# A mixture-of-experts layer whose weights stream through a ring: the large and the small expert of a pair alternate unit by unit within a phase, and the down product waits for its groups of tokens one by one

## The reference, cut to what matters

```
def swiglu(h, w_gate, w_up, w_down):
    return (jax.nn.silu(h @ w_gate) * (h @ w_up)) @ w_down

# 8 experts, w_gate[e], w_up[e]: 1024 x 3584, w_down[e]: 3584 x 1024
# every token goes to its 2 best experts, weighted by its normalised softmax
out[token] += swiglu(x[token], w_gate[e], w_up[e], w_down[e]) * p[token, e]
```

## Time and profile before

| | |
|---|---|
| time, median of 3 runs | 1342.46 us (1342.03 to 1346.38) |
| the profiled execution: its time, its span | 1343.16 us, 1341.3 us |
| PE busy, matmuls | 1277.4 us, 95% of the span |
| expert matmuls begin (L1624); last pair placed (L1678 begins) | 472.77 us; 1321.13 us |
| DMA queue of SP | 456.41 MB, 85.1% of 16 engines |

### The profile page before, as it was taken

One profiled execution on the slowest core, in us unless ns is written; L12 is line 12 of the kernel. 1 busy time (PEld: TensorE's weight loads), 2 busy tenths in 40 slices (PEclk: granted clock), 3 DMA queues, 4 the chain that ended last, 5 costly groups with the idle time before them and its releaser, 6 DMA issues.

```text
span 1341.3 us, 28791 instructions
## 1 busy us (share of the span) xinstructions
PE 1277.4 (95%) x12903; PEld 746.0 (56%) x12904; DVE 219.8 (16%) x597; ACT 124.5 (9%) x247; POOL 36.1 (3%) x125
## 2 busy tenths in 40 slices
PE   7999999999998699999899999999999999999995
PEld 3777788877885433346565534665343555343553
DVE  0299200000005601010110201002010002010002
ACT  2201310000002310000001000001000001000002
POOL 1000100000003200000000000000000000000000
PEclk9899999999999899999999999999999999999998
DMA  9999575556436299999999899999999999999993
GB/s 334 408 402 387 202 277 201 211 174 231 162 121 251 90 406 417 418 420 423 420 407 352 356 365 423 392 381 420 417 418 420 422 419 417 419 418 418 423 419 121
DMA packets 87885, 462.23 MB, mean 345 GB/s; under 512 B 8747, under 2 KB 12119, under 8 KB 52663
## 3 DMA queue, kind: packets, MB, share of 16 engines
q1 hardware_dynamic: 85937, 456.41, 85.1%
q10 hardware_dynamic: 1814, 3.85, 0.8%
HBM read 458.94 MB, written 2.24 MB: 344 GB/s over the span
## 4 chain that ended last, share of the span: by engine, by line
PE 80%; DMA 13%; DVE 2%; issue 2%; POOL 1%; ACT 1%; SPq 0%; DVEq 0%; ACTq 0%; POOLq 0%
PE bank L1624 36%; PE bank L1389 25%; DMA ring<-in_w_exp_down_dram 13%; PE bank L1646 9%; PE bank L1572 2%; PE bank L1358 2%; PE bank L1678 1%; PE bank L1595 1%; PE bank L1286 1%; POOL ROWS L625 1%; SPq L527 0%; DVE xT L957 0%; ACT MIX L890 0%; PE bank L1516 0%; PE bank L1337 0%
## 5 line engine op out<-in xcount | busy, mean ns | idle before, releaser
L1624 PE MATMUL bank<-ring,HT 128*32 128x512 f32 (+1 forms) x5376 | 510.1, 539 | 3.5 <-DMA ring<-in_w_exp_up_dram 3.5
L1624 PEld LDWEIGHTS bank<-ring,HT 128*32 128x32 f32 x5376 | 189.1, 110 | 312.5 <-issue 298.2
L1389 PE MATMUL bank<-HT,ring 128*128 128x264 f32 x1024 | 234.0, 390 | 2.5 <-POOL HT L619 2.5
L1389 PEld LDWEIGHTS bank<-HT,ring 128*128 128x128 f32 x1024 | 195.4, 192 | 43.6 <-issue 10.3
L1646 PE MATMUL bank<-ring,hid_t 128*32 128x256 f32 x2560 | 149.2, 379 | 2.6 <-DMA ring<-in_w_exp_down_dram 2.6
L1646 PEld LDWEIGHTS bank<-ring,hid_t 128*32 128x32 f32 x2560 | 86.2, 110 | 56.3 <-issue 5.6
L1389 PE MATMUL bank<-BIG,ring 128*128 128x264 f32 x480 | 107.3, 386 | 0.0
L1389 PEld LDWEIGHTS bank<-BIG,ring 128*128 128x128 f32 x480 | 91.1, 190 | 15.5
L1646 PE MATMUL bank<-ring,COND 128*32 128x256 f32 x1568 | 89.6, 380 | 9.9 <-DMA ring<-in_w_exp_down_dram 9.7
L1646 PEld LDWEIGHTS bank<-ring,COND 128*32 128x32 f32 x1568 | 50.2, 110 | 47.8 <-DMA ring<-in_w_exp_down_dram 18.5
L1223 DVE TENSOR_TENSOR hid_t<-bank,hid_t 128x512 f32<-128x512 f32 (+1 forms) x22 | 14.2, 643 | 361.0 <-PE bank L1624 360.3
(11 more groups left out here) (230 smaller groups left out, 527.8 us busy)
## 6 DMA issues: line engine op xcount, KB each, us to landing
ring<-in_w_exp_gate_dram SPq DMA_DIRECT2D x64, 1024.0 KB, 15.1
ring<-in_w_exp_up_dram SPq DMA_DIRECT2D x64, 1024.0 KB, 16.2
ring<-in_w_exp_down_dram SPq DMA_DIRECT2D x64, 1024.0 KB, 24.1
ring<-in_w_ada_dram SPq DMA_DIRECT2D x48, 1024.0 KB, 12.9
ring<-in_w_exp_gate_dram SPq DMA_DIRECT2D x64, 768.0 KB, 16.0
ring<-in_w_exp_up_dram SPq DMA_DIRECT2D x64, 768.0 KB, 14.6
ring<-in_w_exp_down_dram SPq DMA_DIRECT2D x32, 1536.0 KB, 25.2
ring<-in_w_in_dram SPq DMA_DIRECT2D x10, 1024.0 KB, 24.9
```

The lines of the kernel that those rows point to most:

```text
L1389: ins = t_.matmul(banks_of[label][:, 0:NT], w[:, k, f * P:(f + 1) * P], src(k0 + k), start=(k0 + k == 0), stop=(k0 + k == k_tiles - 1))
L1624: ins = t_.matmul(bank[GATE_BANKS[role][g]][i * GRP:(i + 1) * GRP, 0:cols], xg[:, k, c0:c0 + GRP], w[:, i, :], start=(k == 0), stop=(k == ...
```

## The change: what it does

Within a phase the units of the two experts alternate by a string of letters, L for the large and S for the small expert: gate LL, then LS six times, then SS; up LLL, LS five times, SSS; down 0 LLLSLLSLLSLS; down 1 LSSLSSLSSLSS. Loads and products follow the same strings, so ring places and the order of use still agree. The transposes move: the large expert's to the small one's up units 6 (three groups) and 7 (the others) in every variant, the small expert's to the large one's units 2 of gate 1 and of down 0. In the first pair the large expert's gate units are issued first, as before, now with holes between them for the small expert's. The down product waits for `hidT` group by group. Sizes, matmuls, transposes, copies and their number stay.

```
-PHASES = tuple((role, kind, HALVES[role][f])
-               for kind, f in (("gate", 0), ("up", 0), ("gate", 1), ("up", 1), ("down", 0), ("down", 1)) for role in ROLES)
+GATE_ORDER = "LL" + "LS" * 6 + "SS"
+UP_ORDER = "LLL" + "LS" * 5 + "SSS"
+DOWN_ORDERS = ("LLLSLLSLLSLS", "LSSLSSLSSLSS")
+PHASES = (("gate", 0, GATE_ORDER), ("up", 0, UP_ORDER), ("gate", 1, GATE_ORDER), ("up", 1, UP_ORDER),
+          ("down", 0, DOWN_ORDERS[0]), ("down", 1, DOWN_ORDERS[1]))
...
-    for role, kind, half in PHASES:
-        for i in DOWN_LOADS[half] if kind == "down" else range(DT):
+    for kind, s, order in PHASES:
+        left = {role: list(DOWN_LOADS[HALVES[role][s]] if kind == "down" else range(DT)) for role in ROLES}
+        for letter in order:
+            role = {"L": "large", "S": "small"}[letter]
+            i, half = left[role].pop(0), HALVES[role][s]
...
+            def first_pair_loads():
+
+                known = [n for n in range(2 * DT) if LOADS[n][0] == "large"]
+                for n in known:
+                    pair_load(n, 0, 0)
+                sp.wait_ge(on("flags_ready"), 1)
+                small = expert_at(1)
+                for n in range(PAIR_LOADS):
+                    if n not in known:
+                        pair_load(n, 0 if LOADS[n][0] == "large" else small, 0)
+
+            def pair_units(large, small, base):
+                for n in range(PAIR_LOADS):
+                    pair_load(n, large if LOADS[n][0] == "large" else small, base)
...
-                    pe.wait_ge(on(f"{role}_hidT"), p * 2 * most + 2 * most)
-                    for u in DOWN_LOADS[half]:
...
+                            if first and jj == 0:
+                                pe.wait_ge(on(f"{role}_hidT"), p * 2 * most + (most + g + 1))
...
-                early, late = (4, 7) if count["small"] == 1 else (3, 5)
-                for s in range(2):
-                    large = [("large", s, g) for g in range(count["large"])]
-                    before_it = [("small", s - 1, g) for g in range(count["small"])] if s else []
-                    expand("large", "gate", s, {3: before_it})
-                    expand("small", "gate", s, {})
-                    expand("large", "up", s, {})
-                    expand("small", "up", s, {early: large[:3], late: large[3:]})
-                down("large", 0, {4: [("small", 1, g) for g in range(count["small"])]})
-                down("small", 0, {})
-                down("large", 1, {})
-                down("small", 1, {})
...
+                turns = {("small", "up", 0, 6): large[0][:3], ("small", "up", 0, 7): large[0][3:],
+                         ("large", "gate", 1, 2): small[0],
+                         ("small", "up", 1, 6): large[1][:3], ("small", "up", 1, 7): large[1][3:],
+                         ("large", "down", 0, 2): small[1]}
+                for kind, s, order in PHASES:
+                    left = {"L": 0, "S": 0}
+                    for letter in order:
+                        role, i = ("large" if letter == "L" else "small"), left[letter]
+                        left[letter] += 1
+                        if kind == "down":
+                            i += DOWN_LOADS[HALVES[role][s]][0]
+                        for turned in turns.get((role, kind, s, i), ()):
                             turn_hid(*turned)
+                        if kind == "down":
+                            down(role, s, i)
+                        else:
+                            expand(role, kind, s, i)
```

More of the change, by code:

```diff
@@ new lines, in pair_load @@
+            def pair_load(n, e, base):
+                role, kind, i, start, size = LOADS[n]
+                at, half = start % (RING * UNIT), int(kind[-1]) if kind != "down" else 0
+                if kind == "down":
+                    src = down_0[e, i // 2, :, (i % 2) * size:(i % 2 + 1) * size] if i < 8 else down_1[e, i - 8]
+                else:
+                    src = (gate_v if kind[0] == "g" else up_v)[e, i, :, SPLIT[half][0]:SPLIT[half][0] + size]
+                end = start + size
+                if n + 1 < PAIR_LOADS and LOADS[n + 1][:3] == ("small", "gate0", 0):
+                    end += LOADS[n + 1][4]
+                if (role, kind, i) != ("small", "gate0", 0):
+                    sp.wait_ge(ring_used, base + (UNITS0 + loads_before(end)))
+                sp.dma_start(ring_flat[:, at:at + size], src).then_inc(expert_loaded[n % LOAD_SEMS], 16)
@@ L1609, in bank_free, with expand @@
                         pe.wait_ge(on("x_updated"), p * DT + 5)
-                def expand(role, kind, s, turns):
+                def expand(role, kind, s, k):
                     cols, groups = SPLIT[HALVES[role][s]][1], count[role]
-                    for k in range(DT):
-                        for turned in turns.get(k, ()):
-                            turn_hid(*turned)
-                        n, w = load(QUAD)
-                        if (role, kind, s) == ("large", "gate", 0) and k % 2 == 0:
-                            pe.wait_ge(on("xg_ready"), p * 4 + (k // 2 + 1))
+                    n, w = load(QUAD)
+                    if (role, kind, s) == ("large", "gate", 0) and k % 2 == 0:
+                        pe.wait_ge(on("xg_ready"), p * 4 + (k // 2 + 1))
+                    for g in range(groups):
+                        if k == 0:
+                            bank_free(role, kind, s, g)
+                        c0 = columns_of(role, g)
+                        for i in range(QUAD):
+                            ins = t_.matmul(bank[GATE_BANKS[role][g]][i * GRP:(i + 1) * GRP, 0:cols],
+                                            xg[:, k, c0:c0 + GRP], w[:, i, :], start=(k == 0), stop=(k == DT - 1))
+                            if n and g == 0 and i == 0:
+                                ins.then_inc(ring_used, 1)
+                        if k == DT - 1:
+                            ins.then_inc(on(f"{role}_{kind}_done"), step_of(g, groups, MOST[role]))
@@ L1619, in expand, with down @@
+                def down(role, s, u):
+                    groups, most, half = count[role], MOST[role], HALVES[role][s]
+                    parts = DOWN_PARTS[u]
+                    n, w = load(parts)
+                    first, last = u == DOWN_LOADS[half][0] and not s, u == DOWN_LOADS[half][-1] and s
+                    for jj in range(parts):
+                        at = (u // 2, 2 * (u % 2) + jj) if half == 0 else (u - 8, jj)
+                        c0 = at[1] * P + at[0] * GRP
                         for g in range(groups):
-                            if k == 0:
-                                bank_free(role, kind, s, g)
@@ L1622, in expand @@
[L1622 removed]
+                            if first and jj == 0:
+                                pe.wait_ge(on(f"{role}_hidT"), p * 2 * most + (most + g + 1))
+                            b = bank[OUT_BANKS[role][g // 2]]
                             for i in range(QUAD):
[L1624 to L1627 removed]
@@ new lines, in down @@
+                                ins = t_.matmul(b[i * GRP:(i + 1) * GRP, (g % 2) * DQ:(g % 2 + 1) * DQ],
+                                                hidT[role, half][g][:, c0:c0 + GRP], w[:, jj, i * DQ:(i + 1) * DQ],
+                                                start=bool(first and jj == 0 and g % 2 == 0),
+                                                stop=bool(last and jj == parts - 1), skip_group_check=True)
+                                if jj == 0 and g == 0 and i == 0:
+                                    ins.then_inc(ring_used, 1)
```

56 lines of the change are left out of this document (9 added, 47 removed).

## The result

The changed kernel takes **1346.13 us** (median of 20 runs, 1341.98 to 1348.81) against 1343.44 (20 runs, 1340.54 to 1348.6) for the kernel before: ratio 1.0022, 95% interval 1.0013 to 1.0031. That is 0.2% slower, inside the 0.3% named as no change and inside the range of 1336 to 1348, but 0.1 us above the likeliest case's 1339.5 to 1346. And the terms gave +0.5 us, where the measurement says +2.7 (by the interval 1.7 to 4.2).

What follows compares the result with a forecast made beforehand. Narrow pairs were taken as bound by DMA, the slim pair 1 by PE. Terms -0.7 + 0.6 + 0.6 = +0.5 us on 1343.16, with the base median 1342.46, gave 1343.0 us; range 1336 to 1348.

Steps and rivals of the forecast that it cites:

- the two large terms: Fuller ring at pair 2's start wins 8.6 us of DMA time; stops of the full ring lose 8.0 us.
- the gap after pair 1: Placing and gather between pair 1 and pair 2, taken over from the earlier trace as 13.54 us.
- Rival C: Half-speed clock stretch after PE's load waits: up to 3.5 us won or lost; bad part, with switch costs, chance 0.03.
- Ring in pair 1: Ring level at pair 1's placing about 10.1 MB instead of 5.4, full before pair 2: 8.6 us of DMA time won.
- Where it is lost again: Around pair 2's start the full ring stops the DMA engines: 6.5 us after the start plus 1.5, in all 8.0.
- The second stop: After the restart in pair 2, the load after the next three waits for ring places: another 1.5 us lost.
- rival A: At pair 2's start the ring only just fills, or engines restart at once; 8.0 us of stops vanish: 1335; chance 0.15.
- The last units: At the ends of DMA-bound pairs 0 and 3, PE finishes later after the last landing: +0.6 us each.
- Transposes, unit switches: Later transposes and added switches between large and small units in the slim pair: 0 each; switches at most 2 us.
- B: Transposes too late at both phase changes of the slim pair, all five copies bare: +6.4 us, 1349.4; chance 0.07.
- Down waits one by one: Down product waiting group by group: 0, at best -1.3 us.
- First pair: Small expert's loads and later-issued early large loads in pair 0, hidden by spare time and idle engines: 0.

Runs made afterwards that it cites:

- e5: The changed kernel with PE's loop over the pairs written out, right for this input alone: 1334.91 us, ratio 0.9937.
- e6: The kernel before with PE's loop over the pairs written out, right for this input alone: 1334.62 us, ratio 0.9935.
- e9: The changed kernel, right for any input, PE's code holding four pairs in line in their likely forms, other forms behind: 1337.75 us, ratio 0.9953.
- e10: The kernel before, right for any input, with PE's four pairs in line in their likely forms, other forms behind: 1337.22 us, ratio 0.9952.
- e4: The kernel before with only the down product's wait changed, from one for all groups to one by one: 1344.02 us, ratio 1.0009.
- e7: The changed kernel with PE's prefetch hint for the branch back moved from the body's start to just ahead of the placing: 1344.43 us, ratio 1.0005.
- e11: The changed kernel again, unchanged, beside the kernel before in the same rounds: 1345.65 us, ratio 1.0017.
- e3: Against the kernel before, only the down phases alternate, with down waits one by one; gate and up keep the old order: 1345.45 us, ratio 1.0010.
- e2: Against the kernel before, only the gate and up phases alternate; down keeps the old order: 1344.07 us, ratio 1.0008.
- e12: The changed kernel with PE's prefetch hint for the branch back put ahead of a pair's last three units: 1344.42 us, ratio 1.0011.
- e1: The kernel before, run once more unchanged: 1343.06 us, ratio 1.0004.

## Why the prediction was right, and where its terms were not

**The verdict held**, no change within 0.3%, though the +2.7 measured lie close to that bound, and what made them up was not in the sum. The sum of the order, +0.5, fits the +0.3 (e5 against e6) and +0.5 (e9 against e10) measured without the branch, each known to 1.1 to 1.4 us. In part that is luck: in these four kernels the ring doesn't fill before pair 2, so the two large terms, -8.6 and +8.0, are of another size there. In the kernels that loop, pair 0 and the rest together are 1.8 us longer with the new order (averages of four profiles against three), and the sum had 0.5 of that. **The term that failed** most is the gap after pair 1, which was counted as a constant. The sum took 17.04 and 13.54 us of the earlier trace rows over as they stood. In the first two profiles its +2.7 are PE's longer idle time at the branch (+0.9) and the stretch at half speed (+1.7). Rival C had named such a stretch and its price, up to +3.5, but tied it to PE's waits for loads, and gave its bad part 0.03. In the gap it came behind the branch, and in e4 with the old order too. So did the stretch of the earlier trace rows that rival C read it from: ahead of it stand the branch at pair 0's end, 2.25 us from 668.17, and 2.64 us in which PE was idle beside it. Of the 3.1 us between the forecast of 1343.0 and the 1346.13, another 1.0 is the base: the median that it went on was that of 3 runs, 1342.46, and that of 20 is 1343.44.

What rival C described is in the traces as well, and costs nothing that can be seen: in e5, e7, e9 and e11, all with the new order of the down units, PE waits 2.1 to 2.5 us for a load near the end of pair 0 and a stretch at 0.50 follows. In e11 the unit's first row takes 1.93 us, the same row of the changed kernel's first profile, behind a shorter wait, 1.07:

```profile
648.90 1.93 PE L1659 MATMUL bank<-ring,hid_t 128*32 128x256 f32 x16 [2.28 <-DMA ring<-in_w_exp_down_dram]
```

```profile
648.71 1.07 PE L1659 MATMUL bank<-ring,hid_t 128*32 128x256 f32 x16 [1.61 <-DMA ring<-in_w_exp_down_dram]
```

Pair 0 is bound by DMA there and lasts as long with the stretch as without (192.6 against 192.5 us).

**Ring in pair 1.** Level at pair 2's start by the prediction's own working: 401.95 us at 403 GB/s are 162.0 MB, 352.3 - 176.2 - 162.0 = 14.1 MB; full, as said (11.1 before). But 16.25 us at 347 GB/s bring 5.6, so the level at pair 1's placing was 8.5, not 10.1. (Summing the queue's packets in the trace, less the units used, gives 14.7 and 9.1, and 6.1 at the placing before.) The fall over the four rounds was as forecast, 10.2 to 9.1 MB by the packets. What was too high is the 11.1 that it started from: the old order reaches that only at the end of its four large units in a row, and held 7.7 ahead of them. Pair 1 itself moved 224.3 x (393 - 381) = 2.7 MB more instead of 4.7. The three windows show the order of it: 357, 397 and 401 GB/s for 341, 327 and 375; the first is barely better, so the 21 us didn't shrink evenly. By the packets, e3 has 8.4 MB at the placing and e2 5.7, so down's order brings 2.3 of the 3.0 MB gained.

**Where it is lost again.** Right in kind, and nearly in size. Of the 8.0 us missing from 917 to 929, 2.8 lie ahead of pair 2's start (324 GB/s up to 920: 0.7; still from there to 922.15: 2.1), 5.2 behind it, where 6.5 were forecast: the refill left SP 3.66 us after the start, as forecast, but the engines ran again 1.6 us later (218 of 419 GB/s from 926 on), not 2.9. The second stop, forecast 1.5: 31 us at 391 GB/s, 2.1. Together 7.3 for 8.0. At a level of 8.5 the ring fills only because the gap is long. In e5 and e9, with a gap of 12.2, it reaches 8.5 + 5.1 = 13.6 MB and just misses: this is rival A's condition. It still gains only 1.0 us in the rest, both times (400.1 against 401.1; 401.4 against 402.3), one profile each. The engines stop for the first refill all the same. So A is out in both its halves: the ring that only just fills didn't bring its 8 us, and an instant restart didn't come.

```profile
915.00:918.00 3.00, 3.00 (x26) 1.65 (x29) 2.09 (x9) 1.79 (x3) 0.00 (x0) 1.00 0.83 339
918.00:921.00 3.00, 3.00 (x32) 0.91 (x28) 0.00 (x0) 0.12 (x1) 0.00 (x0) 1.00 0.19 48
```

(Windows of e9, whose pair 2 begins at 916.28.)

**The last units.** Pair 0: 192.3 to 192.7 us in the profiles of the full change that loop, 191.3 to 192.0 in the kernel before's: +0.8 on average for +0.6. At pair 3's end the forecast pattern is there; the large unit waits, the small ones follow at once:

```profile
1316.72 1.07 PE L1659 MATMUL bank<-ring,hid_t 128*32 128x256 f32 x16 [1.07 <-DMA ring<-in_w_exp_down_dram]
...
1320.63 3.64 PE L1659 MATMUL bank<-ring,COND 128*32 128x256 f32 x64
```

**Transposes, unit switches** (0 and 0): pair 1 lasts 224.1 us with them, 223.9 before, and PE has no idle time in it; B is out, and so is the bound of 2 us. **Down waits one by one** (0): e4's products last as before. **First pair** (0): pair 0's first expert matmul is at 472.0, 472.8 before.

**What stays open**: why the fetch begins earlier ahead of the branch in the kernel before's code. The code's place in the 16 KB blocks is a guess that was not tried. So are the two neighbours of that question: what the packet ahead of the branch holds, and what the branch would do without its hint. That the idle time brings the half-speed stretch is likely, not shown by itself. For it: every such stretch between the first and the last pair stands right behind 2.0 to 2.7 us in which PE was idle; the seven profiles with branches of 1.86 us or more at pair 1's end have two in the gaps (in e2 and e12 the second is behind pair 2), the three with less have none or one, and the four without a looping branch none there. Against it as a rule: e1 has branches of 2.09 and 2.23 us and no stretch, and in e12 PE was idle as long after pair 1 as in the changed kernel, and the rows behind it stay at 0.43:

```profile
911.95 0.53 PE L1590 MATMUL bank<-MIX,ROWS 128*128 128x160 f32 x2 [2.11 <-DVE tmp L976]
...
912.87 0.43 PE L1590 MATMUL bank<-MIX,ROWS 128*128 128x160 f32 x2
```

## What to carry to other kernels

Before an order of loads is tuned by fractions of a microsecond, look at what stands between the stages: a taken branch of PE's queue can cost 2 us while the loads run at 420 GB/s and, in some executions, another 1.7 in clock behind it, and the waits view may name some other engine. Code laid out so that the likely path has no far jump was worth 6 to 8 us here, and without the branch the order of units was worth nothing that could be measured. And where a change fills a ring at the end of a slow stage (here from 6 to 9 MB of 14.7, and full one gap later), take off the stop and the restart at once: most of the gain was given back there.

## What the runs showed of the hardware

- A taken branch back in PE's code ended 2.4 to 2.55 us after the last 16 KB packet of code ahead of it began (packet itself 1.0 to 1.1 us), at 420 GB/s of other loads; seen as 0.98 to 2.29 us of branch. The far branch out of the loop took 3.3 to 3.8 us. A branch on to the code behind it took 75 to 100 ns.
- A prefetch hint at the body's start, 40 to 48 matmuls or 184 to 192 matmuls ahead of the branch made no difference to that. No run is without it.
- Stretches at granted clock 0.50 stood behind 2.0 to 2.7 us of idle PE, at the branch and in waits for loads alike: gather rows of 0.74 instead of 0.43 us, in kernels whose engine work was the same. Twelve idle times of 2.0 to 2.4 us had no such stretch behind them, against twenty that had.
- Two programs that differ in how they wait at down's start (e4 and the kernel before) differ in their profiles by 2.8 us in a gap that lies 70 us behind it, and by 1 us or less in any pair's stretch or other gap. Their times, 1344.02 and 1342.89 us, can't be told apart.
